# Two key tiles of the first attention computed in the delta rule and in the norm behind it, narrower bias strips, and rounded products for 88 merge branches

## What is computed

```python
p = _split_in(x @ w_in[l])
ya = _mixer_a(p["a_q"], p["a_k"], p["a_v"], rpb_table[:, :A_HEADS])
...
yd = _mixer_d(p["d"], d_mu[l], d_w0[l], ...)          # a scan over rows, then a norm over each head
gates = jax.nn.sigmoid(p["gate"].reshape(bsz, seq, N_BRANCHES, D_MODEL))
merged = jnp.sum(gates * jnp.einsum('bsnc,ncd->bsnd', ys, w_branch[l]), axis=2)
...
term = jax.nn.sigmoid(h @ w_gate[l, n]) * (yb @ w_branch[l, n])    # second block, n = 0 to 4
merged = term if merged is None else merged + term
```

## Time and profile before

| | us |
|---|---|
| median of 3 runs (2505.22 to 2509.12) | 2507.2 |
| the profiled execution's own time | 2503.74 |
| its span | 2502.0 |
| mean granted TensorE clock | 0.927 of full |

### The profile page before, as it was taken

How to read it: one execution, slowest core, us unless ns; L and a number is a source line. 1 busy time by engine, 2 the same in 40 slices (tenths; PEclk the granted TensorE clock), 3 DMA queues, 4 the chain that set the end, 5 groups by cost and what they waited for, 6 DMA issues and landing times. The chain is left out here.

```text
span 2502.0 us, 29536 instructions
## 1 busy us (share of the span) xinstructions
PE 2237.3 (89%) x11074; PEld 1629.5 (65%) x11074; DVE 1318.2 (53%) x2300; ACT 858.6 (34%) x1437; POOL 105.3 (4%) x151
## 2 busy tenths in 40 slices
PE   6698998899997899992799989999979998999997
PEld 4487766556766555551677667877757766787776
DVE  2552346856445555553344485953444456777434
ACT  3321233123222565663343232321333334233223
POOL 0000001200000222210000000000000000000000
PEclk8685999999997899996799999999989999999999
DMA  4230432221323899994332212333323222132402
GB/s 143 106 92 2 116 112 63 67 84 61 104 84 135 283 353 348 336 320 167 92 119 69 63 56 68 102 113 101 109 77 113 98 60 64 41 104 85 134 26 110
DMA packets 275291, 299.05 MB, mean 120 GB/s; under 512 B 48845, under 2 KB 247581, under 8 KB 275113
## 3 DMA queue, kind: packets, MB, share of 16 engines
q1 hardware_dynamic: 270026, 288.71, 35.9%
q0 software_dynamic: 5120, 8.40, 1.1%
HBM read 285.75 MB, written 24.69 MB: 124 GB/s over the span
## 5 line engine op out<-in xcount | busy, mean ns | idle before, releaser
L1466 PE MATMUL acc<-x_hi,w_hi 128*128 128x512 f32 x1632 | 682.4, 418 | 22.2 <-DVE w_lo L1419 15.6
L1467 PE MATMUL acc<-x_lo,w_hi 128*128 128x512 f32 x1632 | 646.6, 396 | 0.0
L1468 PE MATMUL acc<-x_hi,w_lo 128*128 128x512 f32 x1632 | 645.8, 396 | 0.0
L1394 ACT CAST w_hi<-raw 128x1024 fp32r<-128x1024 f32 x204 | 212.6, 1043 | 745.9 <-PE acc L1468 695.0
L1419 DVE TENSOR_TENSOR w_lo<-raw,w_hi 128x1024 fp32r<-128x1024 f32 x195 | 238.4, 1224 | 368.3 <-ACT w_hi L1394 361.6
L1466 PEld LDWEIGHTS acc<-x_hi,w_hi 128*128 128x128 f32 x1632 | 312.4, 191 | 109.9 <-issue 28.9
L1467 PEld LDWEIGHTS acc<-x_lo,w_hi 128*128 128x128 f32 x1632 | 312.4, 191 | 77.1 <-issue 14.1
L1468 PEld LDWEIGHTS acc<-x_hi,w_lo 128*128 128x128 f32 x1632 | 311.5, 191 | 70.6
L1476 PE MATMUL br<-y_t,raw_b 128*128 128x512 f32 x448 | 215.7, 604 | 19.6 <-DVE sg L1428 19.6
L1097 DVE TENSOR_TENSOR w_lo<-wgu,w_hi 128x1024 fp32r<-128x1024 f32 x128 | 150.7, 1220 | 126.7 <-ACT w_hi L1056 126.7
L1056 ACT CAST w_hi<-wgu 128x1024 fp32r<-128x1024 f32 x128 | 127.8, 1045 | 109.8 <-DMA wgu<-in_moe_w_up 105.3
(11 more groups left out here) (512 smaller groups left out, 2656.6 us busy)
## 6 DMA issues: line engine op xcount, KB each, us to landing
raw<-in_w_in SPq DMA_DIRECT2D x61, 1024.0 KB, 5.4
raw<-in_w_gate SPq DMA_DIRECT2D x40, 1024.0 KB, 5.1
wgu<-in_moe_w_gate SPq DMA_DIRECT2D x32, 1024.0 KB, 11.5
wgu<-in_moe_w_up SPq DMA_DIRECT2D x32, 1024.0 KB, 14.7
wd<-in_moe_w_down SPq DMA_DIRECT2D x32, 1024.0 KB, 9.5
raw_b<-in_w_branch SPq DMA_DIRECT2D x56, 256.0 KB, 2.6
room<-in_w_out SPq DMA_DIRECT2D x3, 2048.0 KB, 9.1
y_t<-in_w_out SPq DMA_DIRECT2D x3, 2048.0 KB, 10.6
```

Source lines behind the costliest of these rows:

```text
L1394: self.nc.scalar.copy(self.w_hi[:, n % 2], self.weights(n)).then_inc(self.rounded, 1)
L1466: pe.matmul(acc, hi, tile.hi[:, k, :], start=(k == 0), stop=False)
L1467: pe.matmul(acc, hi, tile.lo[:, k, :], start=False, stop=False)
L1468: mm = pe.matmul(acc, lo, tile.hi[:, k, :], start=False, stop=(k == KT - 1))
```

## The change

1. *Key tiles.* A new object LeadTiles does the two key tiles of attention A in four halves of 12 products each. Weights come into y_t[:, 6:10] by two loads of 512 KB on SyncE in delta_scan. ScalarE rounds halves 0 and 1 ahead of step 8 of its 34, and halves 2 and 3 and takes out tile 0 at step 24; VectorE subtracts halves 0 and 1 ahead of its wait for delta_g, 2 and 3 behind the solve. TensorE does halves 0 and 1 behind the memory tiles, ahead of its wait for delta_t. Half 2 stands between the means and the sums of the norm at the start of attention A, half 3 behind the sums. The lead loses its keys.
2. *Strips.* A strip's rows have 640, 640 and 512 numbers instead of 1024. The first two tiles of memory weights are issued in delta_lead.
3. *Branches.* For merge_c and all units of the second block, 88, the branch is six rounded products. ScalarE rounds and VectorE subtracts the branch weights in the step of the gate's tile, into one pair of buffers; the y tile of 8 units likewise, at the first of them. Slots of branch weights: 2 instead of 3.
4. *Stages.* The 16 units of merge_stage in the second block go into conv_stage; the load of w_out beside them goes with them. The gate's product stands at step 1, behind weights(1) and ahead of normalize(0), instead of step 2, and its tanh lies in att.pn. Some small inputs of delta_inputs lie elsewhere, with 16 or 32 rows instead of 64.

```diff
 def bias_tile(scratch, h, i, col, width):
+    first, wide = STRIP[scratch.shape[2]], scratch.shape[2]
...
-                for b, (w, x) in enumerate(((a2, lo), (w2, th), (g2, sg))):
+                for b, (w, x) in enumerate(((a2, lo[0:32]), (w2, th[0:16]), (g2, sg[32:64]))):
...
 # delta_scan, vector
+                for half in range(2):
+                    lead.rest(dve, half)
                 dve.wait_ge(x_in, 48)
...
                 dve.sem_inc(x_ready, 1)
+                for half in (2, 3):
+                    lead.rest(dve, half)
+                dve.wait_ge(lead.split, 4)
                 dve.wait_ge(s_done, 1)
 # scalar
                 for n in range(34):
+                    if n == 8:
+                        for half in range(2):
+                            lead.round(act, half)
                     if n == 24:
...
                         memory.act_values(act, ps)
+                        for half in (2, 3):
+                            lead.round(act, half)
+                        lead.evict(act, ps[:, 5, :], 0)
 # sync
                 for n in (2, 3):
                     memory.load(sp, n)
+                for t in range(2):
+                    lead.load(sp, t)
                 sp.wait_ge(copied, 8)
 # tensor
                 memory.pe_values(pe, ps)
+                for half in range(2):
+                    lead.half(pe, ps[:, 5, :], half)
                 pe.wait_ge(t_in, 32)
...
+class LeadTiles:
+    def half(self, pe, acc, half):
+        pe.wait_ge(self.split, half + 1)
+        for n in range(4):
+            k = 4 * (half % 2) + n
+            hi, lo = self.w_hi[:, half % 2, n, :], self.w_lo[:, half % 2, n, :]
+            pe.matmul(acc, hi, self.x_hi[:, k, :], start=(k == 0), stop=False)
+            pe.matmul(acc, hi, self.x_lo[:, k, :], start=False, stop=False)
+            mm = pe.matmul(acc, lo, self.x_hi[:, k, :], start=False, stop=(k == KT - 1))
+        mm.then_inc(self.used, 1)
+    def evict(self, act, acc, t):
+        act.wait_ge(self.used, 2 * t + 2)
+        self.nc.scalar.copy(self.outs[t], acc).then_inc(self.out, 1)
...
 # DeltaOutput
-    def pe_start(self, pe):
+    def pe_start(self, pe, acc):
         self.norm.pe_means(pe)
+        self.lead.half(pe, acc, 2)
         self.norm.pe_sums(pe)
+        self.lead.half(pe, acc, 3)
...
-    def act_start(self, act):
+    def act_start(self, act, acc):
         self.norm.act_root(act)
+        self.lead.evict(act, acc, 1)
...
 # Stream.load, with B_SLOTS = 2
-                    if b >= self.SLOTS:
-                        sp.wait_ge(self.br_done, 2 * (b - self.SLOTS) + 2)
+                    if b >= self.B_SLOTS:
+                        sp.wait_ge(self.br_done, 2 * (b - self.B_SLOTS) + 2)
...
+class BranchHalves:
+    def round(self, act, tile):
+        u, b, slots = tile.unit, tile.pair, self.stream.B_SLOTS
+        if u:
+            act.wait_ge(self.stream.br_done, u)
+        if u % 8 == 0:
+            self.nc.scalar.copy(self.y_hi[:], tile.row).then_inc(self.y_rounded, 1)
+        act.wait_ge(self.stream.b_in[b % slots], 16 * (b // slots) + 16)
+        self.nc.scalar.copy(self.b_hi[:], self.raw(tile)).then_inc(self.b_rounded, 1)
+    def rest(self, dve, tile):
+        u = tile.unit - self.first
+        if u % 8 == 0:
+            dve.wait_ge(self.y_rounded, u // 8 + 1)
+            self.nc.vector.tensor_tensor(self.y_lo[:], tile.row, self.y_hi[:].bitcast(F32), ALU.subtract).then_inc(self.split, 1)
+        dve.wait_ge(self.b_rounded, u + 1)
+        self.nc.vector.tensor_tensor(self.b_lo[:], self.raw(tile), self.b_hi[:].bitcast(F32), ALU.subtract
+                                     ).then_inc(self.split, 1)
+    def pe(self, pe, acc, tile):
+        u = tile.unit - self.first
+        pe.wait_ge(self.split, u + 1 + u // 8 + 1)
+        for k in range(2):
+            hi, lo = self.b_hi[:, k, :], self.b_lo[:, k, :]
+            pe.matmul(acc, hi, self.y_hi[:, k, :], start=(k == 0), stop=False)
+            pe.matmul(acc, hi, self.y_lo[:, k, :], start=False, stop=False)
+            mm = pe.matmul(acc, lo, self.y_hi[:, k, :], start=False, stop=(k == 1))
+        return mm
...
 # attention_stage, vector
                 for s in range(steps):
-                    if gate is not None and s == 2:
+                    att.weights(dve, s)
+                    if gate is not None and s == 1:
                         dve.wait_ge(th_ready, 1)
...
 # delta_lead, sync
                 for n in tiles:
                     stream.load(sp, n + 2)
+                for n in range(2):
+                    memory.fetch(sp, n)
                 sp.wait_ge(copied, 6)
...
-            keys, values, queries = (stream.project(w_in, n, 2, x_hi, x_lo) for n in (256, 512, 0))
+            values, queries = (stream.project(w_in, n, 2, x_hi, x_lo) for n in (512, 0))
...
-                    conv_stage(c, stream, [*conv[4:14], *of_rest[0]], glu[:], ...)
-                c.load_beside([(h_room, of("w_out_2")[:, 0:512].rearrange("(k p) n -> p k n", p=P))])
-                merge_stage(c, stream, [*of_rest[1], *of_rest[2]])
+                    c.load_beside([(h_room, of("w_out_2")[:, 0:512].rearrange("(k p) n -> p k n", p=P))])
+                    conv_stage(c, stream, [*conv[4:14], *of_rest[0], *of_rest[1], *of_rest[2]], glu[:], ...)
...
-    dram = {"strips_a": scratch("strips_a", (4, P, 1024)), "strips_b": scratch("strips_b", (4, P, 1024)),
-            "strips_w": scratch("strips_w", (4, P, 1024)), ...
+    dram = {"strips_a": scratch("strips_a", (4, P, 640)), "strips_b": scratch("strips_b", (4, P, 640)),
+            "strips_w": scratch("strips_w", (4, P, 512)), ...
```

More of the change, by code:

```diff
@@ L40 @@
 MEM = 256
+STRIP = {640: 0, 512: 256}
 EXPERT_SLOTS = 3
@@ L365, in _, with delta_scan @@
                 mm.then_inc(summed, 1)
-def delta_scan(c, r, k, v, kk, sig_w, a, y, scratch, eye, room_u0, room_st, memory):
+def delta_scan(c, r, k, v, kk, sig_w, a, y, scratch, eye, room_u0, room_st, memory, lead):
     nc, NG = c.nc, 2 * NCD
@@ L594, in _ @@
                 for h in range(4):
+                    if h == 3:
+                        pe.wait_ge(lead.out, 1)
                     for ch in range(8):
@@ L1370, in load @@
             units = sum(t.unit is not None for t in self.tiles[:splits - 1])
[L1371 removed]
+            if any(group == j and 2 * (b - self.B_SLOTS) + 2 > units for b, (group, _) in enumerate(self.pairs)):
                 return
@@ L1393, in round @@
             act.wait_ge(self.acc_done, n - 1)
-        self.nc.scalar.copy(self.w_hi[:, n % 2], self.weights(n)).then_inc(self.rounded, 1)
+        self.nc.scalar.copy(self.w_hi[n % 2], self.weights(n)).then_inc(self.rounded, 1)
     def evict(self, act, n):
@@ L1414, in act, with halved @@
             self.evict(act, n - 1)
+        if self.halved(n):
+            self.halves.round(act, self.tiles[n])
+    def halved(self, n):
+        return self.halves is not None and self.tiles[n].unit is not None
     def rest(self, wait, eng, n):
@@ L1452, in dve @@
             self.mix(dve, n - 1)
+        if self.halved(n):
+            self.halves.rest(dve, self.tiles[n])
     def pool(self, pool, n):
@@ L1611, in turned, with __init__, raw, close @@
             self.nc.scalar.copy(self.pt[:, e, 0:w], self.tps[:, e, 0:w]).then_inc(self.t_out, 1)
+class BranchHalves:
+    def __init__(self, c, ctx, stream, first):
+        self.c, self.nc, self.stream, self.first = c, c.nc, stream, first
+        self.y_hi, self.y_lo = (c.sb(ctx, x, [P, 2, S], F32R) for x in ("y_hi", "y_lo"))
+        self.b_hi, self.b_lo = (c.sb(ctx, x, [P, 2, P], F32R) for x in ("b_hi", "b_lo"))
+        self.y_rounded, self.b_rounded, self.split = (c.held_sem(x) for x in ("y_rounded", "b_rounded", "b_split"))
+        stream.halves = self
+    def raw(self, tile):
+        return self.stream.raw_b[:, tile.pair % self.stream.B_SLOTS, :, tile.at:tile.at + P]
+    def round(self, act, tile):
[17 more added lines that the diff above has]
+        pe.wait_ge(self.split, u + 1 + u // 8 + 1)
+        for k in range(2):
+            hi, lo = self.b_hi[:, k, :], self.b_lo[:, k, :]
[3 more added lines that the diff above has]
+        return mm
+    def close(self):
+        self.c.fresh += [self.y_rounded, self.b_rounded, self.split]
 def spread(tiles, steps):
@@ L1633, in attention_stage @@
         beside += [[], []]
-        turn_after = lead[2 * many + 1] if many else None
+        ahead = many if earlier is None else 0
+        turn_after = lead[ahead + many + 1] if many else None
         rows_ps = att.tps[:].rearrange("p b s -> p (b s)")
@@ L1657, in _ @@
                 if earlier is not None:
-                    earlier.pe_start(pe)
+                    earlier.pe_start(pe, stream.br[:])
                 for n in lead:
@@ L1663, in _ @@
                     if many and n == turn_after:
-                        pe.wait_ge(stream.freed, lead[2 * many - 1] + 1)
```

(14 more changed lines are left out.)

118 lines of the change are left out of this document (77 added, 41 removed).

## The result

The changed kernel takes **2463.8 us** (median of four runs, 2459.0 to 2468.0); beside it the kernel before took 2507.1 (2505.2 to 2509.1). The ratio is 0.9827, 95% interval 0.9807 to 0.9847. The profiled execution took 2462.61, span 2460.8, against 2503.74 and 2502.0: 41.1 less, where 36.1 was forecast.

A forecast was written before the change was run, and what follows sets the result against it. The prediction took TensorE, busy for 89% of the span, to bound the kernel. Its terms summed to -36.1 us, from the profiled 2503.74 to 2467.6, or 2471.1 against the median of 2507.2; range 2460 to 2485.

The forecast's parts named there:

- the forecast's own case: Whole kernel: the terms hold and the time falls at 2465 to 2478 us; chance 0.56.
- Branches: Merge units: six rounded products save 0.34 us per unit, -24.5 over 72 units; the two hgrn stages lose, +3.8.
- the rival of a longer branch: 72 units: two float32 products take eight spacings, 1.83 us, so each unit wins 0.46; 2462 us, chance 0.05.
- Strips and fetch: SyncE stuck no longer: -3.1 us after strips_w, -3.1 at delta_scan's opening, -4.1 at its first products.
- First key tile: Delta rule: 24 products behind the memory tiles hide delta_t; 3.6 us late, 1.9 back by the clock, +1.8.
- Second key tile: First attention: two tiles leave the lead, -11.2 us; lead starts 14.2 in, +2.1; together -9.1.
- Barrier: Between conv stage and merges: TensorE's idle 0.99 us at the barrier goes, twice, -2.0.
- Gate's product: Ahead of normalize(0): delays TensorE's first turn by about 1.05 us in each of four stages, +4.2.
- Two slots, fewer rows: Branch weights issued 14 us ahead of use, against 2.6 to land, and fewer rows in delta_inputs: both cost nothing.
- the new work lands on the path: Rival: first attention's low clock +5.8, hgrn taking all VectorE work +5.2, delta rule's key tile +2.3; 2484 us, chance 0.20.
- the split is late everywhere: Rival: all 88 branches wait for refill and split of the one b pair; +43, 2550 us, chance 0.04.
- more is won: Rival: gate's step hidden -4.2, all hgrn units gain -9.2, clock up in the lead -2.2; 2456 us, chance 0.13.

The follow-up runs named there:

- e1: Changed kernel with all 88 split branches back to two plain float32 products: 2487.9 us, against 2463.8.
- e2: Changed kernel with only the 16 branches of the two hgrn stages back to plain products: 2463.6 us, against 2463.8.
- e5: Changed kernel with all 64 rows again in the three low-rank products of delta_inputs: 2465.4 us, against 2463.8.
- e9: Changed kernel with strips 1024 wide again and the first two memory weight loads issued behind them, in the stage of delta_inputs: 2473.1 us, against 2463.8.
- e6: Changed kernel with strips 1024 wide again, memory weights still issued ahead of them: 2464.3 us, against 2463.8.
- e7: Changed kernel with the first two memory weight loads issued in the stage of delta_inputs again, behind the narrow strips: 2466.3 us, against 2463.8.
- e8: Changed kernel with ScalarE rounding the lead's first weights before it evicts the second key tile, in the first attention: 2456.9 us, against 2463.8.
- e4: Kernel of e1 with the gate's product back in step 2, in a buffer of its own: 2488.4 us, against 2487.9 for e1.
- e3: Changed kernel with GpSimd instead of VectorE doing the split's subtractions in the hgrn stages: 2464.4 us, against 2463.8.

## Why the prediction held, and where its terms did not

The median of 2463.8 lies inside the stated range and 1.2 us below 2465 to 2478, the forecast's own case. The sum of the terms was 36.1, the two profiled executions differ by 41.1.

1. **Branches.** Forecast -24.5 and +3.8. Measured -25.6 (e1) and +4.0 (e2). Two errors cancel: the usual spacing is 0.2267 and not 0.229, so that the plain branch took 7.21 - 24 x 0.2267 = 1.77 and the split one takes 1.36, 0.41 less in a merge tile; in the attention, conv and merge_c stages a unit gives only 0.28 to 0.35. So the rival of a longer branch (0.46 per unit) was half right: 0.41 lies between it and my 0.34. The Trainium skill's page "FP8 and Floating Point Precision", section TensorE Precision Notes, has a float32 product as four passes; for two products that is 8 spacings, 1.81, and the trace's 1.77 nearly agrees. The split was ready in time everywhere off the hgrn stages, as worked out. In them the size was right in part by luck. The term started from 2.14 us as the longest wait before a branch, which is that of the first of the two stages; the second has 3.80 in the kernel before. And it had no share for the clock, which is down longer behind the longer wait (windows in e2).
2. **Strips and fetch.** Forecast -3.1, -3.1 and -4.1, 10.3 in all. The stretch to the first products is 12.5 shorter; less the 1.6 of e5, 10.9. (Without taking the fewer rows off, e9 gives 12.3: the two overlap, so 10.9 is one way to share the 12.5 out, and one profile's.) The size and the places were right, as was what held SyncE. The step that failed is the attribution, "in the next stage SyncE is stuck in the memory weights behind the strips": taken as two gains from two edits, where e6, e7 and e9 show that the second 3.1 and the 4.1 come with either edit alone. The first 3.1, too, is lost only in e9 (56.2, against 54.3 in e6 and 54.4 in e7): it takes wide strips and a late start of them, and in e6 they started early.
3. **First key tile.** Forecast 3.6 late and 1.9 back, +1.8. Measured: L602 starts 53.2 us behind the first products instead of 49.6 and takes 2.1 less; +1.5. Right, and the reason given, that the products behind start under the higher clock, is what the 14 profiles show.
4. **Second key tile.** Forecast -9.1 and a lead 14.2 us in; measured 14.3 in and -7.6 (-7.4 to -9.9 over the profiles). The order and the wait of about 3 us were as forecast. Missed, and of the size of the whole shortfall: behind that wait the granted clock is down for most of the lead's first 3.7 us, where nine products stand 0.43 apart and not 0.23, 1.7 us in all; e8 shows that it need not be.
5. **Barrier.** -2.0, measured -2.4 (e1 against the kernel before, with 0.4 of it not traced to the barrier).
6. **Gate's product.** +4.2, measured +2.3 (e4; up to +3.2). Failed: "Four stages". The row was of windowed attention, and I took it for memory attention too, where VectorE has the time.
7. **Two slots, fewer rows.** "In delta_inputs fewer rows enter under the same columns: nothing" failed: -1.6 (e5). It was judged by the work of one product, and the gain lies between two products. The Trainium skill's page "TensorEngine Tiling (Array Packing)", section Key Properties, says that different tiles of the array can run matmuls in parallel; e5 agrees (3.6 us against 7.0).

With these, -25.6 + 4.0 - 10.9 + 1.5 - 7.6 - 2.4 + 2.3 - 1.6 = -40.3; the rest, 0.8, is left open; it is less than the clock moves single stages by. The rivals "the new work lands on the path" and "the split is late everywhere" are refuted, the first by stages that came within 1.5 us of their terms, the second by the merge period. Of "more is won" only half of the gate's step came true; neither hgrn units nor the clock in the lead gave anything.

## What to carry to other kernels

Ask of each stall that a change removes whether a second edit of the same change would remove it alone: two covers for one stall are counted once. Compare stages rather than totals where unchanged code can meet either level of the granted clock; five runs did not separate kernels that a single timeline separates, and a stage too has to be compared with one under the same clock. And where an engine's wait ends a burst of TensorE work, price the wait with what follows at the lower clock: 1.7 us behind the 2.88 in the lead.

## What the runs showed of the hardware that was not expected

- Float32 products on rows 0 to 15 and on rows 32 to 63 ran side by side: 3.6 us for eight of 512 columns, against 7.0 with 64 rows each (e5), all at 1.2 GHz.
- Subtractions with two SBUF inputs on VectorE and GpSimd at once held one another up for about as long as they overlapped: VectorE's 1.23 became 1.82, GpSimd's small one 0.72 became 1.71. GpSimd's large one went from 2.4 to 3.46 beside a VectorE scaling with one SBUF input (e3).
- The granted clock was down for 6.8 us behind the first branch of an hgrn stage where TensorE had waited 5.7 us for it (13 stages) or 4.1 (one), and for 3.4 where it had waited 2.06 to 3.80, in 9 stages of 10.
- The first 15 us of delta_scan's products ran at 1.00, or from 0.6 to 2.3 us on at 0.50 of the clock, in different profiles of unchanged code; the memory tiles behind them came 20.7 to 21.5 us in with the former, 26.2 to 27.5 with the latter.
